# A two-block network on one core: stick-breaking weights from two sigmoids and a scan over the keys, in place of log-softplus, triangular products and an exponential

## The reference, cut to what matters

```python
def stick_breaking_attention(q, k, v):
    for i in range(s_len // BLOCK):          # BLOCK = 128, s_len = 512
        end = (i + 1) * BLOCK
        z = jnp.einsum('bhtd,bhsd->bhts', q[block i], k[:end]) * scale    # scale 1/8
        mask = s_pos[None, :] < t_pos[:, None]
        log_1m_beta = jnp.where(mask, jax.nn.log_sigmoid(-z), 0.0)
        after = lax.cumsum(log_1m_beta, axis=3, reverse=True) - log_1m_beta
        log_a = jax.nn.log_sigmoid(z) + after
        a = jnp.where(mask, jnp.exp(log_a), 0.0)
        outs.append(jnp.einsum('bhts,bhsd->bhtd', a, vb))
```

## Time and profile before

| | |
|---|---|
| median of 3 runs | 2000.9 us (2000.25 to 2002.14) |
| the profiled execution's own time | 2000.74 us |
| span of its trace | 1998.8 us |
| mean granted TensorE clock | 0.987 of full |
| busy: PE, PEld, DVE, ACT, POOL | 97%, 75%, 44%, 36%, 26% of the span |
| matmul records on PE | 8805 |
| the eight pairs run | from 62.7 to about 304 us |

### The profile page before, as it was taken

One profiled execution on the slowest core, in us unless ns is written; L12 is line 12 of the kernel. 1 busy time (PEld: TensorE's weight loads), 2 busy tenths in 40 slices (PEclk: granted clock), 3 DMA queues, 4 the chain that ended last, 5 costly groups with the idle time before them and its releaser, 6 DMA issues.

```text
span 1998.8 us, 21930 instructions
## 1 busy us (share of the span) xinstructions
PE 1931.1 (97%) x8805; PEld 1508.0 (75%) x8805; DVE 886.0 (44%) x1473; ACT 712.7 (36%) x1057; POOL 510.3 (26%) x285
## 2 busy tenths in 40 slices
PE   7989999999999999998999999998999999999998
PEld 6666667887877787887888888876675678888886
DVE  6465560446254203325333333557736654433433
ACT  5655473132323232333222222424435432222223
POOL 4322224444444443330000000133335501100100
PEclk9999999999999999999999999999999999999999
DMA  9311112453434121422523331422121123232221
GB/s 303 100 43 63 43 43 84 137 189 106 147 127 148 64 85 63 139 94 73 150 69 100 105 98 59 124 85 63 57 71 64 43 95 97 94 99 91 85 97 51
DMA packets 182332, 192.22 MB, mean 96 GB/s; under 512 B 10154, under 2 KB 166064, under 8 KB 182104
## 3 DMA queue, kind: packets, MB, share of 16 engines
q1 hardware_dynamic: 179704, 180.84, 28.1%
q0 software_dynamic: 1104, 4.98, 1.0%
q10 hardware_dynamic: 1424, 5.00, 0.7%
HBM read 188.69 MB, written 4.72 MB: 97 GB/s over the span
## 4 chain that ended last, share of the span: by engine, by line
PE 86%; DVE 9%; ACT 2%; issue 1%; POOL 0%; DMA 0%; SPq 0%; DVEq 0%; POOLq 0%; ACTq 0%
PE bank L1454 23%; PE bank L1455 22%; PE bank L1457 22%; PE bank L1476 2%; PE bank L1475 2%; PE bank L1474 2%; PE bank L1559 2%; DVE spl L1828 2%; DVE tmp L1822 1%; PE bank L1515 1%; PE bank L1529 1%; PE bank L1545 1%; DVE sph L1826 1%; PE bank L1484 1%; DVE zs L1815 1%
## 5 line engine op out<-in xcount | busy, mean ns | idle before, releaser
L2578 POOL TENSOR_TENSOR wl<-stg,wh 128x1024 fp32r<-128x1024 f32 x150 | 360.2, 2402 | 921.2 <-ACT wh L2223 921.2
L1454 PE MATMUL bank<-hH,wh 128*128 128x512 f32 x1264 | 523.9, 414 | 7.0 <-ACT q L2258 4.2
L1455 PE MATMUL bank<-hL,wh 128*128 128x512 f32 x1264 | 505.5, 400 | 0.0
L1457 PE MATMUL bank<-hH,wl 128*128 128x512 f32 x1264 | 505.4, 400 | 0.0
L2223 ACT ACTIVATE wh<-stg 128x1024 fp32r<-128x1024 f32 (+2 forms) x292 | 298.2, 1023 | 300.2 <-PE bank L1457 219.5
L1454 PEld LDWEIGHTS bank<-hH,wh 128*128 128x128 f32 x1264 | 241.7, 191 | 84.2 <-issue 26.6
L1457 PEld LDWEIGHTS bank<-hH,wl 128*128 128x128 f32 x1264 | 241.0, 191 | 58.8
L1455 PEld LDWEIGHTS bank<-hL,wh 128*128 128x128 f32 x1264 | 242.2, 192 | 51.3 <-issue 0.7
L1766 DVE TENSOR_TENSOR wl<-stg,wh 128x1024 fp32r<-128x1024 f32 (+2 forms) x142 | 168.1, 1186 | 238.0 <-ACT wh L2223 237.5
L1454 PE MATMUL bank<-h2H,wh 128*128 128x512 f32 x352 | 140.9, 400 | 0.0
L1455 PE MATMUL bank<-h2L,wh 128*128 128x512 f32 x352 | 140.2, 398 | 0.0
(11 more groups left out here) (334 smaller groups left out, 2762.4 us busy)
## 6 DMA issues: line engine op xcount, KB each, us to landing
stg<-in_w_in SPq DMA_DIRECT2D x54, 1024.0 KB, 5.2
stg<-in_w_ffn_in SPq DMA_DIRECT2D x22, 1024.0 KB, 5.1
stg<-in_w_ada SPq DMA_DIRECT2D x16, 1024.0 KB, 5.4
stg<-in_w_ffn_gate SPq DMA_DIRECT2D x11, 1024.0 KB, 5.1
stg<-in_w_ffn_up SPq DMA_DIRECT2D x11, 1024.0 KB, 5.1
stg<-in_w_ffn_down SPq DMA_DIRECT2D x10, 1024.0 KB, 5.0
stg<-in_w_ada SPq DMA_DIRECT2D x16, 512.0 KB, 6.7
stg<-in_w_proj_ret SPq DMA_DIRECT2D x8, 1024.0 KB, 5.0
```

Of the source, the lines that this page charges most:

```text
L1454: T.matmul(ps, wh, xh, start=j["first"] and k == 0, stop=False)
L1455: T.matmul(ps, wh, xl, start=False, stop=False)
L1457: t = T.matmul(ps, wl, xh, start=False, stop=j["stop"] and last)
L2578: G.tensor_tensor(lo, src, hi, ALU.subtract).then_inc(s["w_lo_pool"], 1)
```

## The change

The scores are now made with the queries on the partitions and all keys up to the block's end along the free dimension (q is the stationary operand, k the moving one). The five tiles hold the same number of columns as before. Per tile:

- ACT: sigmoid(-z) into tmp, and sigmoid(z) over the score (`sba`, two instructions in place of three).
- DVE: `sbr`, a running product of sigmoid(-z) from the last key to the first by `tensor_tensor_scan` with a negative step, one scan per block (so two in tiles 0, 1, 2), and then a product of it, shifted by one key, with sigmoid(z). This takes the place of `sbsp` and of the addition L1832.
- PE: `sbt`, four 128x128 transposes of the tile, so that keys are on the partitions for the product with v. It takes the place of `sbc`.
- ACT: `sbe` copies them out of the bank, in place of the Exp.
- `sbo`: 20 matmuls of 64x128 in place of 8 of 64x512, 384, 256, 128 columns.

The triangle and -1 matrices, their conversion, and the reloads of an ACT table after each gate_sb job go away. The masks gain an all-zero row that serves as the scan's addend, and are 1024 KB in place of 768 KB. `attend` is written anew: 33 steps a pair in place of 22.

```diff
-PATS = [(2, [(0, 2, 0), (1, 2, 256)]), (1, [(0, 1, 0), (0, 3, 384)]), (1, [(1, 1, 0), (1, 3, 384)]),
-        (0, [(0, 0, 0)]), (0, [(1, 0, 0)])]
+PATS = [(2, [(0, 1, 0), (1, 1, 256)]), (1, [(0, 2, 0), (0, 0, 384)]), (1, [(1, 2, 0), (1, 0, 384)]),
+        (0, [(0, 3, 0)]), (0, [(1, 3, 0)])]
...
-        def left(n):
-            take("C", ("sbc", pr, n))
-            emit("sbc", pr, n)
-            give(("sbc", pr, n))
+        def turned(n):
+            take("C", ("sbt", pr, n))
+            emit("sbt", pr, n)
+            yield
+            emit("sbe", pr, n)
+            give(("sbt", pr, n))
+
         scores(0)
+        yield from rest(3)
+        emit("sba", pr, 1)
+        yield from rest(2)
+        emit("sba", pr, 2)
+        scores(1)
+        yield from rest(2)
+        emit("sbr", pr, 1)
+        yield from rest(2)
+        emit("sba", pr, 0)
         yield
...
+        emit("sbr", pr, 2)
         yield
         scores(2)
+        yield from turned(1)
         yield
+        emit("sbr", pr, 0)
         emit("sba", pr, 3)
-        emit("sbsp", pr, 0)
+        yield from rest(2)
+        yield from turned(2)
         yield
         emit("sba", pr, 4)
         yield
...
+        emit("sbr", pr, 3)
+        yield from turned(0)
+        yield from rest(2)
+        emit("sbr", pr, 4)
+        yield from rest(2)
+        yield from turned(3)
+        yield from rest(3)
+        yield from turned(4)
+        yield from rest(2)
...
-    def tables_again(f):
-        if p.fore:
-            emit("tables", f)
...
-                        t = T.matmul(zb[hh][:, off:off + w], kt[64 * hh:64 * hh + 64, j * P:(j + 1) * P],
-                                     qt[64 * hh:64 * hh + 64, j * P:S], start=True, stop=True)
+                        t = T.matmul(zb[hh][:, off:off + w], qt[64 * hh:64 * hh + 64, i * P:(i + 1) * P],
+                                     kt[64 * hh:64 * hh + 64, 0:w], start=True, stop=True)
...
-                            t = T.matmul(cb[:, off + w - w2:off + w], TRI if jj == j else NEG1, sp_[nn][:, o2:o2 + w2],
-                                         start=jj == j and part == 0, stop=jj == 3 and part == 1)
-                t.then_inc(fill(("sbc", pr, n)), 1)
+            def sbt(pr, n):
+                pe.wait_ge("sbr", 2 * nth["sbr", pr, n])
+                turn(("sbt", pr, n), ZS[n])
...
+                for i in range(4):
+                    for j in range(i + 1):
+                        for hh in range(2):
+                            n, off = WHERE[hh, i]
+                            t = T.matmul(ob[64 * hh:64 * hh + 64, i * P:(i + 1) * P], vt[:, j * P + 64 * hh:j * P + 64 * hh + 64],
+                                         AT[n][:, off + j * P:off + (j + 1) * P], start=j == 0, stop=j == i)
...
-                V.scalar_tensor_tensor(tt[:, :], ZS[n][:, :], 0.0, tt[:, :], ALU.max, ALU.add).then_inc(s["sbsp"], 1)
...
-                V.tensor_copy(SPH[n][:, :], tt[:, :]).then_inc(s["sbsp"], 1)
...
-                V.tensor_tensor(SPL[n][:, :], tt[:, :], SPH[n][:, :], ALU.subtract).then_inc(s["sbsp"], 1)
...
-                V.tensor_tensor(ZS[n][:, :], cb[:, :], ZS[n][:, :], ALU.add).then_inc(empty(("sbc", pr, n)), 1)
+                for _, i, off in PATS[n][1]:
+                    e = off + P * (i + 1)
+                    back = slice(e - 1, off - 1 if off else None, -1)
+                    t = V.tensor_tensor_scan(left[:, back], tt[:, back], masks[:, 3, back], 1.0, ALU.mult, ALU.add)
+                t.then_inc(s["sbr"], 1)
+                ve.wait_ge("sbr", 2 * c - 1)
+                ve.wait_ge("sba", 2 * c)
+                V.tensor_tensor(ZS[n][:, 0:S - 1], ZS[n][:, 0:S - 1], left[:, 1:S], ALU.mult).then_inc(s["sbr"], 1)
...
-                A_.activation(tt[:, :], ZS[n][:, :], ACTF.Abs).then_inc(s["sba"], 1)
-                ac.wait_ge("sba", 3 * i + 1)
-                A_.activation(tt[:, :], tt[:, :], ACTF.Exp, scale=-1.0).then_inc(s["sba"], 1)
-                ac.wait_ge("sba", 3 * i + 2)
-                A_.activation(tt[:, :], tt[:, :], ACTF.Ln, bias=1.0).then_inc(s["sba"], 1)
...
+                A_.activation(tt[:, :], ZS[n][:, :], ACTF.Sigmoid, scale=-1.0).then_inc(s["sba"], 1)
+                ac.wait_ge("sba", 2 * i + 1)
+                A_.activation(ZS[n][:, :], ZS[n][:, :], ACTF.Sigmoid).then_inc(s["sba"], 1)
...
+                A_.activation(AT[n][:, :], cb[:, :], ACTF.Copy).then_inc(empty(("sbt", pr, n)), 1)
```

More of the change, by code:

```diff
@@ L358, in attend @@
         if pr == 0:
[L359 removed]
+            emit("tables", "sb")
         def scores(g):
@@ L365, in scores, with rest @@
                 give(("sbz", pr, g, hh))
-        def left(n):
-            take("C", ("sbc", pr, n))
-            emit("sbc", pr, n)
-            give(("sbc", pr, n))
-        scores(0)
-        yield
[L373 to L382, removed]
+        def rest(m):
+            for _ in range(m):
+                yield
+        def turned(n):
+            take("C", ("sbt", pr, n))
+            emit("sbt", pr, n)
+            yield
+            emit("sbe", pr, n)
+            give(("sbt", pr, n))
+        scores(0)
+        yield from rest(3)
[7 more added lines that the diff above has]
+        emit("sba", pr, 0)
+        yield
+        emit("sbr", pr, 2)
         yield
         scores(2)
+        yield from turned(1)
         yield
+        emit("sbr", pr, 0)
         emit("sba", pr, 3)
-        emit("sbsp", pr, 0)
+        yield from rest(2)
+        yield from turned(2)
         yield
@@ L1066 @@
 d_bias0 d_bias1 d_bias2 d_bias3 d_gfb d_out
-v_set cact ada pe_ada a_x v_x v_a1 a_n1 v_mats sba sbsp sbe v_rot p_rot v_rs a_rsq p_rsq a_spread v_spread v_rn v_gr
+v_set cact ada pe_ada a_x v_x v_a1 a_n1 sba sbr v_rot p_rot v_rs a_rsq p_rsq a_spread v_spread v_rn v_gr
 a_sq v_sq pe_sum v_a2 v_n2 v_m1 v_extra v_x3 v_sc v_best a_gb v_gc a_gd v_gd a_ge p_gf a_gg p_gh a_gh p_gi
@@ L1139, in program @@
             ZS = [sb(f"zs{i}", [P, S], ctx=ph) for i in range(5)]
-            SPH = [sb(f"sph{i}", [P, S], F32R, ctx=ph) for i in range(5)]
-            SPL = [sb(f"spl{i}", [P, S], F32R, ctx=ph) for i in range(5)]
+            AT = [sb(f"at{i}", [P, S], ctx=ph) for i in range(5)]
+            LEFT = [sb(f"left{i}", [P, S], ctx=ph) for i in range(2)]
         with ExitStack() as ph:
@@ L1496, in sbz @@
                 zb = [free(pe, ("sbz", pr, g, hh)) for hh in range(2)]
-                for e, (j, off) in enumerate(SECS[g]):
-                    w = S - P * j
+                for e, (i, off) in enumerate(SECS[g]):
+                    w = P * (i + 1)
                     for hh in range(2):
-                        t = T.matmul(zb[hh][:, off:off + w], kt[64 * hh:64 * hh + 64, j * P:(j + 1) * P],
-                                     qt[64 * hh:64 * hh + 64, j * P:S], start=True, stop=True)
+                        t = T.matmul(zb[hh][:, off:off + w], qt[64 * hh:64 * hh + 64, i * P:(i + 1) * P],
+                                     kt[64 * hh:64 * hh + 64, 0:w], start=True, stop=True)
                         if e == len(SECS[g]) - 1:
                             t.then_inc(fill(("sbz", pr, g, hh)), 1)
[L1505 to L1514, removed]
-                            t = T.matmul(cb[:, off + w - w2:off + w], TRI if jj == j else NEG1, sp_[nn][:, o2:o2 + w2],
-                                         start=jj == j and part == 0, stop=jj == 3 and part == 1)
-                t.then_inc(fill(("sbc", pr, n)), 1)
+            def sbt(pr, n):
+                pe.wait_ge("sbr", 2 * nth["sbr", pr, n])
+                turn(("sbt", pr, n), ZS[n])
             def sbo(pr):
@@ L1523, in sbo @@
                 ob = free(pe, ("sbo", pr))
[L1524 to L1530, removed]
+                for n in range(5):
+                    emptied(pe, ("sbt", pr, n))
+                for i in range(4):
[4 more added lines that the diff above has]
+                                         AT[n][:, off + j * P:off + (j + 1) * P], start=j == 0, stop=j == i)
                 t.then_inc(fill(("sbo", pr)), 1)
```

86 lines of the change are left out of this document (31 added, 55 removed).

## The result

The changed kernel takes 1951.56 us (median of 4 runs, 1950.54 to 1952.63), the kernel before beside it 2001.52. The ratio is 0.9751, with a 95% interval from 0.9734 to 0.9768. The span of the profiled execution is 1948.7 us against 1998.8.

What follows compares the result with a forecast made beforehand. The prediction took PE, busy 97% of the span, as the bound. PE's work -19.3, waits -9.4 and the first pair -6.9 summed to -35.6 us, from 2000.74 to 1965 us; eight-in-ten range 1953 to 1984.

Steps and rivals of the forecast that it cites:

- PE's work: PE in the eight pairs: sums removed, transposes added, product with v slightly dearer, scores unchanged; -19.3 us.
- Transposes: Four transposes per turned tile on PE, 0.42 us plus 0.09 and 0.08 around them; 22.4 us added in all.
- Sums over keys: PE's products at L1515, taken out: 5.3 us a pair, with tile 0 set at 0.93; -42.5 us.
- Waits: PE's waits for DVE in the pairs: old ones 19 us, new ones 9.6 us, net -9.4 us.
- its 1 us of room at tile 0: DVE finishes tile 0's `sbr` after 8.35 us, PE reaches its transposes after 9.35 us.
- the meeting with POOL: DVE stands still during POOL's 2.4 us weight part, once in most pairs; 1.4 us wait there, 1.2 a pair taken.
- The first pair: PE's 4.4 us wait for ACT's copy of q2 and 2.5 us lost to half clock both go; -6.9 us.
- the queue on ACT: First pair: q2's copy stands behind six ACT instructions in place of 15, 3.8 us against 9.5, so no wait.
- the 33 steps: 33 steps a pair are 264; 208 slots give 270, so the last pair ends in time, nothing left uncovered.
- Slow scans: Rival: backward scans on DVE cost twice the forward, 2.45 us; 2028 us; slower or about equal had chance 0.06.
- The clock in the pairs: Rival: PE's clock falls to half in the pairs, 3.4 us lost each time; 1979 to 1992 us, chance 0.08.
- No waits at all: Rival: DVE stays ahead and PE never waits at turned tiles; 1955 us, range 1948 to 1958, chance 0.10.

Runs made afterwards that it cites:

- E5: Changed kernel with each tile's four transposes made twice into the same bank, 160 more transposes: 1963.5 us, ratio 0.9819.
- E1: Kernel before's arithmetic (log-softplus, triangular products, Exp) at the new pace of 33 steps a pair: 1982.2 us, ratio 0.9907.
- E6: Changed kernel, but POOL makes only 16 of 128 columns of each low weight part in jobs beside the pairs: 1946.04 us, ratio 0.9726.
- E2: Kernel before, with the first pair's scores of tiles 3 and 4 and all that follows two steps later: 1999.92 us, ratio 0.9995.
- E3: Changed kernel's arithmetic at the old pace of 22 steps, turned tiles where the sums over keys stood: 1984.4 us, ratio 0.9917.
- E9: Old arithmetic at 33 steps a pair, with the low parts left out of the sums over keys: 1969.5 us, ratio 0.9842.
- E4: Kernel before (22 steps a pair) with the low parts left out of the sums over keys, 160 fewer matmuls: 2001.64 us, ratio 1.0001.

## Why the prediction was partly right

**The step that failed** is the sizing of two terms: PE's work, above all the price of a turned tile, and the waits. The bound and the signs were right: PE bound the stretch and does so still. But the range of 1953 to 1984 did not hold 1951.6. Of the 12.7 us by which the stretch fell further than forecast, 8.9 are PE's work (-30.7 for sums, turned tiles, product, scores and slots, against -19.3 and the 2.5 of half clock), and 3.8 are waits (-13.2 against -9.4).

**Transposes: the term that was sized worst**, +22.4 against +15.2. Three things were wrong. I added 0.09 us for the way in, from 211.20 to 211.53 in the earlier trace rows, 3.6 us for 40 tiles; but that is the way into the product with v, and a turned tile starts 0.23 us after its slot, as the row at 101.84 shows. I took 0.42 for the four transposes, from a block behind the product with v; directly behind a slot they take 0.35, and 15.2 / 40 = 0.38 on the mean. And I charged the way out, 3.2 us, to the tile, where it is real but stands in the row of slots in the table, while I left the way out of the old sums (0.05 each, from 86.22 to the next start) out of theirs, so that the comparison was uneven. I had transposes that follow a slot in the same trace, at 70.90, 0.24 us after the matmul ahead of them; they show that there is no way in. E5 gives 0.106 us for each further transpose.

**Sums over keys**, -42.5 against -45.0 (43.0 at full clock, E1). The set value for tile 0 and the price by rows 3 were close; 2.0 of the missing 2.5 us are that the first pair's sums ran at half clock, which the forecast put into another line.

**Waits.** The old ones were 19.6 against 19 by my reading, the new ones 6.4 against 9.6. The trace of DVE's chain, its 1 us of room at tile 0 and the meeting with POOL were right, and E6 shows that no wait is left without the meetings. What was wrong is how often and how far they reach PE. There were 11 meetings, more than one a pair, but two of the eight pairs have no wait and a third has 0.4 us; the longest wait is 1.05 us by the modelled end, 1.2 by distances, where I took 1.2 as the mean of all pairs. And I let the other tiles go free, while 2.5 of the 6.4 us stand at tiles 1 and 3.

**The first pair.** -6.9 was right in size: the wait of 4.4 and the half clock are gone. The reason was only half right. I took the queue on ACT alone for the cause; E2 removed that queue in front of q2 by two steps and gained 2 us in a place and lost them in the next. The new pace alone takes nearly all of the wait away: E1, with the old three instructions a tile, has 0.5 us there. The shorter list alone does not: E3, with the new arithmetic at the old pace, waits 3.1 us.

**What the sum could not hold.** I added terms as if each stood by itself. At the new pace they do so in large part (E9: 12.7 us for 21.4 of work; E5: 12 for 17); E4 shows that at the old pace half of the largest term, 18 us less at the sums, was worth 0. The forecast had the 33 steps only as a question of whether the last pair is finished in time. In fact they are 19 us of the gain on their own, and the condition for nearly 14 more. In my sum a part of that stood without its name, as shorter waits. The same arithmetic without its schedule gains 16.8 us (E3), 33 less than with it.

**The rivals.** Slow scans did not occur: 1.22 us backward. The clock in the pairs did not fall at this pace. It did fall in E3 five times, in E4 seven times and in E9 once, each time at a wait or just behind one, so that this rival was real and was averted where the waits became short; my argument against it, that waits of 2.1 us had left the clock alone, was too weak. No waits at all (1955) was the nearest of the rivals, but for another reason: 6.4 us of waits stayed and the work was cheaper.

## What to carry to other kernels

Work beside a bound engine's main stream has two prices, its instructions on that engine and the distance to the engines that feed it, and cutting the first without widening the second can give nothing (E4) while three fifths of the same cut pay with wider spacing (E9). So measure arithmetic and pace apart, each alone and both together. And read the price of an instruction from a place with the same neighbours: the way in depends on what it follows.

## What the runs showed of the hardware

- In the stretch of the pairs every fall to half clock came at a wait of PE or within 2 us of its end, and lasted 3.4 or 6.8 us (E3: five falls, mean 0.95 over 253 us; E4: seven, 0.93 over 270 us). The length of the wait does not decide it by itself: one of 1.8 us was followed by a fall (E9 at 87 us), while one of 2.4 us (E2 at 74 us) and one of 1.8 were not. Nor does their distance: in E3 the clock fell behind a wait of 2.1 us at 129.3 with no other in the 24 us before it, and stayed at full through waits of 1.8 and 2.1 us that end 4 us apart, at 216.4 and 220.3. What decides between them was not found. The windows of these two places in E3:

```profile
216.00:224.00 8.00, 5.49 (x43) 4.42 (x44) 4.18 (x3) 3.45 (x7) 2.41 (x1) 1.00 0.00 0
128.00:137.00 9.00, 6.94 (x24) 5.27 (x25) 5.42 (x4) 3.40 (x6) 2.38 (x1) 0.62 0.01 2
```

- The falls cost 17 us in E4, which together with longer waits made a saving of 18 us at the sums void.
- A transpose of 128x128 fp32 in a row of them costs PE 0.106 to 0.109 us and showed no effect on the granted clock, at 160 or at 320 in the stretch.
- A `tensor_tensor_scan` with a negative step takes as long as one forward, 1.22 us for 512 columns.
- POOL's weight part of 2.4 us holds up a scan as it holds up a two-input product; over the stretch the meetings that E6 takes away cost DVE 19 us, and PE all of its 6.4 us of waits.
